# mLSTM scores as five single-pass products: operands split by heads, output gates loaded later

## The chip, the cores and the metric

The kernel runs on one core of one Trainium2 chip. The metric is the device time of one execution in microseconds (us); less is better. Several executions are timed and their median is given, and one execution is profiled, from which the page and the rows below come.

## The reference, cut to what matters

The program is one layer of a hybrid trunk: a big input projection, three groups of heads (latent attention, bidirectional mLSTM, neighbourhood attention), an output projection, and a convolutional feed-forward network. Only the mLSTM heads are touched. There are 4 of them, with 192 features each, 512 latent tokens (the queries) and 768 keys (512 latent, 256 of context):

```python
q = heads(qk[..., :ML_W])                       # B, 4, S, 192
k = heads(qk[..., ML_W:]) * (ML_DH ** -0.5)
...
a = jnp.einsum('bhtd,bhsd->bhts', qc, kc) * w_loc      # scores times decay weights
num = ... + jnp.einsum('bhts,bhsv->bhtv', a, vc)
den = ... + a.sum(axis=-1)
h = num / jnp.maximum(jnp.abs(den), jnp.exp(-m_t))[..., None]
...
return (h.transpose(0, 2, 1, 3).reshape(o.shape) * o)  # output gate, both directions summed
```

The kernel doesn't scan in chunks. It forms each head's whole scores k·q once, multiplies them by the decay weights of both directions, and sums over the keys. Everything is float32. A product of two float32 operands can be made either by TensorE's own float32 matmul, or by splitting each operand in a high part of the reduced type fp32r and a low part (the rest), and summing fp32r products.

## The kernel before, in words

`stage_front` makes the input projection and writes it to DRAM (`proj`, feature rows by 768 tokens). `stage_mix` has `stage_mla` (latent operands) and `stage_heads`, which runs three parts in one block: `one` (a `softmax` of 6 latent heads, 24 units of 128 queries), `two` (`mlstm`), and `three` (`windows`, neighbourhood attention). `stage_tail` then makes the output projection and the feed-forward network. Each engine has its own instruction list, in an order written by hand, and semaphores tie them.

**Units of mLSTM.** `two` has 24 units: head `n // 6`, and within a head the key tiles in `ORDER` (4, 5, 0, 1, 2, 3): two context tiles and four latent ones. Unit n goes like this:

- SyncE, `load_rows(n)` (L1656): two DMAs bring decay rows, broadcast over 128 partitions, from `rrow` into slot n % 5 of `g_ring`. It first waits until unit n - 5 is done (`v_ok`).
- GpSimd adds the causal mask for latent tiles (`mask`, L1681). Within head 2 it also makes the bias slabs of neighbourhood attention (`extra`, L1273), once their tables have landed.
- ScalarE, `weights(n)` (L1702): two exponentials on the slot. `scalar` (L1714) runs it three units ahead; at the last unit of a head it does `scaled` (L1712) after it: four scaled copies out of the accumulators.
- TensorE, `score(n)` (L1795): the 192 features as two float32 matmuls of 96 rows each, 512 queries wide, into one of two banks. It waits for DVE's products of unit n - 2.
- VectorE, `products(n)` (L1760 for context tiles, L1765 for latent ones): score times weights, into the slot.
- TensorE, `values(n)` (L1818): the slot against the values, 8 blocks for a context tile and 5 for a latent one, each 193 columns wide.

TensorE's list is score(n + 2), values(n), and so on. At the end of a head VectorE makes the inverse denominators (`inverse`, L1727 to L1731), ScalarE scales one direction (L1712) and VectorE adds the other (`summed`, L1740); values of the next head wait for both, since they use the same accumulators. Two units later TensorE turns the head (`turn`, L1806), and VectorE multiplies it by the output gates (`gated`, L1751), which `put` stores.

**Loads.** All of these are on SyncE's one queue. At the start of `stage_heads` it loads q and k of all heads (L1169), the values, and the rows of units 0 to 4. When the latent heads are finished it loads the output gates `l_o` (L1180; q, k and gates lie 96 features to a partition set), and then, in a loop over n from 5, the rows of unit n, followed from n = 6 on by two items of `parts` each: neighbourhood q, two halves of k, a window table and eight bias tables `n_slab_wide` (L1195). A bias table is made of runs of 192 bytes.

Of the kernel before, what the change touches and what calls it, by code (L numbers as in the profile page):

```python
# [764 lines left out]
def stage_mix(nc, A, sb, ps, sem, proj, vtok, mix, ones, eps, front, spent, ends, lat, early):  # L765

    rrow = nc.dram_tensor("rrow", [2 * ML_H, KEYT, SEQ], F32, kind="Internal").ap()
    with ExitStack() as ctx:
# [5 lines left out]
        ml = dict(q=arena.at("l_q", [HALF, 2 * ML_H, SEQ], ML_AT + 40960),  # L774
                  k=arena.at("l_k", [HALF, 2 * ML_H, TOK], ML_AT),
# [344 lines left out]
def stage_heads(nc, A, arena, ps, sem, proj, vtok, mix, ident, ones, rqs, rows_st, mla, ml, na, early):  # L1120

    with ExitStack() as ctx:
# [40 lines left out]
        with nc.Block() as block:  # L1163
            @block.sync
            def _(sp):
                sp.wait_ge(rows_st, 32)
                for dst, at, w in ((ml["q"], O_MQ, SEQ), (ml["k"], O_MK, TOK)):
                    r = row_of(at)
                    sp.dma_start(dst[:, :, :], proj[r:r + ML_W, 0:w].rearrange("(a p) t -> p a t", p=HALF)).then_inc(ml_ld, 16)  # L1169
# [10 lines left out]
                sp.dma_start(ml["og"][:, :, :], proj[r:r + ML_W, 0:SEQ].rearrange("(a p) t -> p a t", p=HALF)).then_inc(og_ld, 16)  # L1180
# [8 lines left out]
                for n in range(SLOTS_R, two.UNITS):  # L1189
# [27 lines left out]
            def _(pe):  # L1217
                def to_mlstm(u):
                    if u == 0:
                        pe.wait_ge(ml_ld, 16 * (2 + KEYT))  # L1220
                        pe.wait_ge(one.e_ok, one.UNITS)
# [19 lines left out]
            def _(dve):  # L1241
                one.vector(dve)
# [38 lines left out]
            def _(act):  # L1281
# [9 lines left out]
                one.scalar(act, head_out, drain)  # L1291
# [29 lines left out]
def softmax(nc, arena, at, sem, tag, heads, score, v, scale, ident, lag, s_ps, t_ps, o_ps):  # L1321
# [66 lines left out]
    def vector(dve):  # L1388
# [12 lines left out]
        for u in range(UNITS + lag):  # L1401
# [8 lines left out]
            if u < UNITS:  # L1410
                inverse(u)

# [7 lines left out]
    def scalar(act, head_out, drain):  # L1420
# [17 lines left out]
        for u in range(UNITS + lag):  # L1438
# [8 lines left out]
            if u >= lag:  # L1447
                turn_and_out(u)
        out(heads - 2)
# [153 lines left out]
def mlstm(nc, arena, sem, ml, banks, ident):  # L1603
# [5 lines left out]
    q, k, og, v = ml["q"], ml["k"], ml["og"], ml["v"]  # L1609
# [7 lines left out]
    HALF_BANK = SEQ // 2  # L1617

# [26 lines left out]
    z_ok = sem("g_ones_set")  # L1645
    mk_ok = sem("g_masked")
# [9 lines left out]
    def load_rows(sp, n):  # L1656
# [4 lines left out]
        for d in (1, 0):  # L1661
# [4 lines left out]
            at += w  # L1666

# [38 lines left out]
    def scalar(act):  # L1706
# [46 lines left out]
    def vector(dve):  # L1753
# [14 lines left out]
        for n in range(UNITS):  # L1768
            products(n)
            h, i = n // KEYT - 1, n % KEYT  # L1770
            if h >= 0:
# [3 lines left out]
                elif i == 2:  # L1775
                    gated(dve, h)
        inverse(dve, ML_H - 1)
# [12 lines left out]
    def score(pe, n):  # L1790
# [41 lines left out]
    f.score, f.turn = score, turn  # L1832
    f.tensor, f.vector, f.gpsimd, f.scalar = tensor, vector, gpsimd, scalar
# [1095 lines left out]
```

## Time and profile before

| | us |
|---|---|
| median of 3 timed runs | 2611.5 (2609.99 to 2613.75) |
| profiled execution, its own time | 2612.05 |
| its span in the profile | 2610.4 |
| latent heads (`one`) | 778 to 880 |
| mLSTM (`two`), first score after the latent heads to last values | 880.8 to 975.6 |
| neighbourhood attention (`three`) | 975.6 to 1027 |
| output projection and feed-forward network | 1027 to the end |

The profiled execution's time is 1.65 us more than its span: what lies around it. How the views are read: a row of the timeline is a start, a length, an engine, a line of the kernel, an operation, output and inputs, and how many instructions are merged; brackets give the idle time of that engine just before and what ended it. The start of one group on TensorE to the start of the next is what the group costs; its own length is longer, since matmuls are pipelined. [...] A float32 matmul shows as two records, an fp32r one as one.

### The profile page before, as it was taken

To read this page: it belongs to the slowest core of one execution; us is meant where nothing else is said; L and a number is where in the kernel's file an instruction comes from. 1 tells how busy PE (TensorE), PEld (TensorE's weight loads), DVE (VectorE), ACT (ScalarE), POOL (GpSimd) and SP (SyncE) were. 2 spreads that over 40 slices of the span, in tenths; PEclk is the share of its full clock that TensorE was granted. 3 is DMA by queue.
4 is the path that set the end of the run, shared out by engine and by line. 5 is a ranking of instruction groups with operands and counts; after the bars stand their busy time and mean duration, and the time that the engine had idled before them with its cause. 6 is when DMAs were issued, how large, how long until landed. Compare 5 with 4: busy or idle time off the path is not lost.

```text
span 2610.4 us, 39575 instructions
## 1 busy us (share of the span) xinstructions
PE 2530.5 (97%) x15352; PEld 2184.3 (84%) x15352; DVE 1553.0 (59%) x1811; ACT 932.0 (36%) x1235; POOL 187.8 (7%) x247
## 2 busy tenths in 40 slices
PE   4999999999999998999999999999999999999997
PEld 3788888888756576888899999999999988888886
DVE  5534543474274336337788888888888854333345
ACT  3221212222334334225455555555555532222222
POOL 1000000000106223000000000000000010000000
PEclk9999999999999999999999999999999999999998
DMA  9855555786405554432322322233223262423223
GB/s 367 328 216 214 208 194 196 259 312 231 147 14 138 129 126 160 172 121 93 125 114 109 136 113 112 108 134 115 112 109 133 107 239 88 144 99 133 100 89 109
DMA packets 109081, 401.48 MB, mean 154 GB/s; under 512 B 17512, under 2 KB 37912, under 8 KB 78280
## 3 DMA queue, kind: packets, MB, share of 16 engines
q1 hardware_dynamic: 79328, 294.78, 32.1%
q0 software_dynamic: 15680, 88.28, 9.0%
q10 hardware_dynamic: 14000, 17.44, 1.8%
q8 instruction: 47, 0.77, 0.1%
q14 instruction: 26, 0.21, 0.0%
HBM read 362.22 MB, written 37.45 MB: 153 GB/s over the span
## 4 chain that ended last, share of the span: by engine, by line
PE 56%; DVE 2%; DMA 1%; ACT 1%; issue 0%; POOL 0%; DVEq 0%; ACTq 0%
PE f_ps L2711 25%; PE f_late_ps L2768 13%; PE f_ps L2768 11%; PE f_first_ps L2768 7%; DMA f_raw<-in_w_down 0%; DVE h L2677 0%; PE f_late_ps L2735 0%; PE f_ps L2722 0%; DVE f_lo L2353 0%; DVE x_lo L2529 0%; DVE f_lo L2433 0%; DVE h L2523 0%; PE f_first_ps L2787 0%; DVE f_c L2478 0%; DMA f_raw<-in_w_up 0%
## 5 line engine op out<-in xcount | busy, mean ns | idle before, releaser
L2711 PE MATMUL f_ps<-f_u_hi,f_hi 128*128 128x512 f32 x671 | 262.9, 392 | 1.7 <-DVE f_lo L2353 1.7
L2711 PE MATMUL f_ps<-f_u_hi,f_lo 128*128 128x512 f32 x671 | 262.7, 392 | 0.0
L2711 PE MATMUL f_ps<-f_u_lo,f_hi 128*128 128x512 f32 x671 | 262.5, 391 | 0.0
L2456 DVE SCALAR_TENSOR_TENSOR h<-f_ps,mod,h 128x512 f32<-128x512 f32 (+1 forms) x76 | 57.0, 751 | 316.4 <-PE f_ps L2711 316.4
L619 PE MATMUL i_ps<-hn_hi,i_hi 128*128 128x512 f32 x608 | 240.5, 395 | 0.0
L619 PE MATMUL i_ps<-hn_hi,i_lo 128*128 128x512 f32 x608 | 239.7, 394 | 0.0
L619 PE MATMUL i_ps<-hn_lo,i_hi 128*128 128x512 f32 x608 | 238.5, 392 | 0.0
L2107 ACT ACTIVATE f_hi<-f_raw 128x1408 fp32r<-128x1408 f32 (+1 forms) x82 | 123.0, 1500 | 295.3 <-PE f_ps L2711 274.1
L2433 DVE TENSOR_TENSOR f_lo<-f_s,f_hi 128x1024 fp32r<-128x1024 f32 x160 | 195.5, 1222 | 41.1 <-ACT f_hi L2137 41.1
L493 DVE TENSOR_TENSOR i_lo<-i_raw,i_hi 128x2048 fp32r<-128x2048 f32 x38 | 87.0, 2291 | 218.3 <-ACT i_hi L357 218.3
L2137 ACT ACTIVATE f_hi<-f_s 128x1024 fp32r<-128x1024 f32 x160 | 168.6, 1054 | 80.3 <-PE f_late_ps L2768 36.4
L2353 DVE TENSOR_TENSOR f_lo<-f_raw,f_hi 128x1408 fp32r<-128x1408 f32 (+1 forms) x82 | 145.9, 1779 | 58.2 <-ACT f_hi L2107 57.8
L2137 ACT ACTIVATE f_hi<-f_raw 128x1024 fp32r<-128x1024 f32 x120 | 126.8, 1058 | 131.0 <-PE f_ps L2768 65.4
L2433 DVE TENSOR_TENSOR f_lo<-f_raw,f_hi 128x1024 fp32r<-128x1024 f32 x120 | 146.8, 1224 | 10.5 <-ACT f_hi L2137 9.0
L2711 PEld LDWEIGHTS f_ps<-f_u_hi,f_hi 128*128 128x128 f32 x671 | 126.0, 188 | 30.3 <-DVE f_lo L2353 1.8
L2711 PEld LDWEIGHTS f_ps<-f_u_hi,f_lo 128*128 128x128 f32 x671 | 126.0, 188 | 27.9
L2711 PEld LDWEIGHTS f_ps<-f_u_lo,f_hi 128*128 128x128 f32 x671 | 126.0, 188 | 27.8
L505 DVE SCALAR_TENSOR_TENSOR i_ring<-i_ring,cs 128x2048 f32<-128x2048 f32 x60 | 138.2, 2346 | 0.0
L619 PEld LDWEIGHTS i_ps<-hn_hi,i_hi 128*128 128x128 f32 x608 | 114.2, 188 | 27.7 <-issue 1.7
L2768 PE MATMUL f_ps<-x_hi,f_hi 128*128 128x256 f32 x480 | 135.8, 283 | 1.4 <-DVE f_c L2439 1.4
L2768 PE MATMUL f_late_ps<-x_hi,f_hi 128*128 128x256 f32 x480 | 135.9, 283 | 0.0
L2768 PE MATMUL f_late_ps<-x_lo,f_hi 128*128 128x256 f32 x480 | 135.8, 283 | 0.0
(413 smaller groups left out, 6658.7 us busy)
## 6 DMA issues: line engine op xcount, KB each, us to landing
f_raw<-in_w_up SPq DMA_DIRECT2D x88, 1024.0 KB, 5.1
i_ring<-in_ada_rest POOLq DMA_DIRECT2D x64, 1024.0 KB, 5.3
f_raw<-in_w_down SPq DMA_DIRECT2D x64, 704.0 KB, 4.0
i_raw<-in_w_in SPq DMA_DIRECT2D x38, 1024.0 KB, 4.9
i_ring<-in_ada_first SPq DMA_DIRECT2D x32, 1024.0 KB, 7.4
f_raw<-in_w_out SPq DMA_DIRECT2D x16, 1024.0 KB, 4.9
u_spill<-f_u SPq DMA_DIRECT2D x44, 256.0 KB, 2.1
f_u_raw<-u_spill POOLq DMA_DIRECT2D x44, 256.0 KB, 5.7
```

Of the source, the lines that this page charges most:

```text
L493: nc.vector.tensor_tensor(w_lo[s][:, :, :], raw[s][:, :, :], w_hi[s][:, :, :].bitcast(F32), ALU.subtract).then_inc(lo_ok, 1)
L505: nc.vector.scalar_tensor_tensor(acc[g], ada[g % 2], col, acc[g], ALU.mult, ALU.add).then_inc(ada_ok, 1)
L619: mm = nc.tensor.matmul(pt[s][:, 0:SEQ], w[s][:, k, :], x[:, k, 0:SEQ], **flags)
L2107: nc.scalar.activation(w_hi[s][:, 0:kt, :], raw[s][:, 0:kt, :], ACT.Copy).then_inc(hi_ok, 1)
L2137: nc.scalar.activation(slot_of(w_hi, q), source(par, q), ACT.Copy).then_inc(bh_ok, 1)
L2353: nc.vector.tensor_tensor(w_lo[s][:, 0:kt, :], raw[s][:, 0:kt, :], w_hi[s][:, 0:kt, :].bitcast(F32), ALU.subtract).then_inc(lo_ok, 1)
L2433: nc.vector.tensor_tensor(slot_of(w_lo, q), source(par, q), slot_of(w_hi, q).bitcast(F32), ALU.subtract).then_inc(bl_ok, 1)
L2456: nc.vector.scalar_tensor_tensor(ht, pt[s][:, :], mod[:, bass.ds(group * KT + m, 1), 0:1].rearrange("p a b -> p (a b)"), ht, ALU.mult, ALU ...
L2711: mm = nc.tensor.matmul(pt[s][:, :], m[:, k, :], v(k, slice(0, SEQ)), start=(k == 0 and n == 0), stop=(k == len(ks) - 1 and n == 2))
L2768: mm = nc.tensor.matmul(to[:, 0:HALF_T], w[:, k, :], v, start=(q in (0, 1, 3) and k == 0 and n == 0), stop=(k == HK - 1 and n == 2), skip_ ...
```

## The change

- The score of a unit is five fp32r matmuls, each 128 rows deep and 512 wide. The first 128 features take three: high·high, high·low, low·high. The last 64 features take two: the key's tail is laid twice over the 128 partitions (high in one tile, low in another), and query's high and low tails are stacked in one tile.
- Operands come by heads. `load_operands(h)` makes six DMAs per head (for q and for k: 128 rows, and the 64 tail rows twice). Heads 0 and 1 are loaded at the start of the stage. Head 2 is loaded after the rows of unit 5 (the latent heads' buffers are its place), and head 3 after the rows of unit 9. Between head 3's first query DMA and its other five, SyncE waits until VectorE is finished with head 2's low parts, since the two heads share one tile.
- Per head ScalarE makes four high parts (`operand_high`) and VectorE four low parts (`operand_low`). For heads 0 and 1 they go between the units of the latent heads (`aside`), for head 2 on ScalarE after its iterations 3 to 6 of mLSTM and on VectorE after its iterations 4 to 7, for head 3 after 9 to 12 and 10 to 13.
- The output gates are loaded after the rows of unit 6, rather than ahead of those of unit 5. The neighbourhood loads begin after the rows of unit 11, rather than 6.

```diff
@@ stage_heads, block.sync
-                for dst, at, w in ((ml["q"], O_MQ, SEQ), (ml["k"], O_MK, TOK)):
-                    r = row_of(at)
-                    sp.dma_start(dst[:, :, :], proj[r:r + ML_W, 0:w].rearrange("(a p) t -> p a t", p=HALF)).then_inc(ml_ld, 16)
+                for h in range(2):
+                    two.load_operands(sp, h, proj)
...
-                sp.dma_start(ml["og"][:, :, :], proj[r:r + ML_W, 0:SEQ].rearrange("(a p) t -> p a t", p=HALF)).then_inc(og_ld, 16)
+                gates = (ml["og"][:, :, :], proj[r:r + ML_W, 0:SEQ].rearrange("(a p) t -> p a t", p=HALF), og_ld)
...
-                    if n >= SLOTS_R + 1:
-                        for dst, src, s in parts[2 * (n - SLOTS_R - 1):2 * (n - SLOTS_R)]:
+                    if n == SLOTS_R:
+                        for m in range(2):
+                            sp.wait_ge(one.stored[m], 16 * (MLA_H // 2))
+                        two.load_operands(sp, 2, proj)
+                    if n == SLOTS_R + 1:
+                        sp.dma_start(gates[0], gates[1]).then_inc(gates[2], 16)
+                    if n == SLOTS_R + 4:
+                        two.load_operands(sp, 3, proj)
+                    if n >= SLOTS_R + 6:
+                        for dst, src, s in parts[2 * (n - SLOTS_R - 6):2 * (n - SLOTS_R - 5)]:
                             sp.dma_start(dst, src).then_inc(s, 16)
...
@@ block.vector, block.scalar: called at the end of each unit of the latent heads
+                def aside(u):
+                    if 12 <= u < 20:
+                        two.operand_low(dve, (u - 12) // 4, (u - 12) % 4)
...
+                def aside(u):
+                    if 11 <= u < 19:
+                        two.operand_high(act, (u - 11) // 4, (u - 11) % 4)
...
@@ mlstm
-    ho = [arena.at(f"g_head{n}", [HALF, 2, SEQ], WORK_AT + 10240 + 4096 * n) for n in range(2)]
+    ho = [arena.at(f"g_head{n}", [HALF, 2, SEQ], WORK_AT + 9280 + 4096 * n) for n in range(2)]
...
+    def load_operands(sp, h, proj):
+        for full, dup, at, w in ((parts[h]["q"], parts[h]["qt"], O_MQ, SEQ), (parts[h]["k"], parts[h]["kt"], O_MK, TOK)):
+            r = row_of(at) + h * ML_D
+            sp.dma_start(full[:, :], proj[r:r + P, 0:w]).then_inc(qk_ld[h], 16)
+            if h == ML_H - 1 and w == SEQ:
+                sp.wait_ge(ql_ok, 4 * h)
+            for n in range(2):
+                sp.dma_start(dup[TAIL * n:TAIL * (n + 1), :], proj[r + P:r + ML_D, 0:w]).then_inc(qk_ld[h], 16)
+
+    def operand_high(act, h, n):
+        o = parts[h]
+        to, frm = ((o["k_hi"], o["k"]), (o["q_hi"], o["q"]), (o["kt_hi"], o["kt"]), (o["qt_st"], o["qt"]))[n]
+        if n == 0:
+            act.wait_ge(qk_ld[h], 96)
+        nc.scalar.activation(to[:, :], frm[:, :], ACT.Copy).then_inc(qh_ok, 1)
+
+    def operand_low(dve, h, n):
+        o = parts[h]
+        dve.wait_ge(qh_ok, 4 * h + n + 1)
...
@@ scalar
+            if n in SPLIT_AT:
+                operand_high(act, *SPLIT_AT[n])
+
+    SPLIT_AT = {n: (2, n - 3) for n in range(3, 7)}
+    SPLIT_AT.update({n: (3, n - 9) for n in range(9, 13)})
@@ vector
+            if n - 1 in SPLIT_AT:
+                operand_low(dve, *SPLIT_AT[n - 1])
@@ score
-        for a in range(2):
-            mm = nc.tensor.matmul(s_ps[n % 2], k[:, 2 * h + a, st * P:(st + 1) * P], q[:, 2 * h + a, :],
-                                  start=(a == 0), stop=(a == 1))
+        if n % KEYT == 0:
+            pe.wait_ge(ql_ok, 4 * (h + 1))
+        o, at = parts[h], slice(st * P, (st + 1) * P)
+        terms = ((o["k_hi"], o["q_hi"]), (o["k_hi"], o["q_lo"]), (o["k_lo"], o["q_hi"]), (o["kt_hi"], o["qt_st"]), (o["kt_lo"], o["qt_st"]))
+        for m, (a, b) in enumerate(terms):
+            mm = nc.tensor.matmul(s_ps[n % 2], a[:, at], b[:, :], start=(m == 0), stop=(m == len(terms) - 1))
```

## Rows read from the trace of the kernel before

**Rows 1.** The page's part 1, TensorE and the others: busy us, share, instructions.

```profile
PE 2530.5 (97%) x15352; PEld 2184.3 (84%) x15352; DVE 1553.0 (59%) x1811; ACT 932.0 (36%) x1235; POOL 187.8 (7%) x247
```

**Rows 2.** Stages: stretch, length, busy PE, PEld, DVE, ACT, POOL, clock, DMA, GB/s.

```profile
778.00:866.00 88.00, 86.63 (x378) 57.77 (x378) 38.63 (x93) 37.10 (x71) 50.76 (x23) 1.00 0.41 110
882.00:922.00 40.00, 35.58 (x151) 27.12 (x150) 11.19 (x25) 10.79 (x23) 4.69 (x7) 0.91 1.07 216
```

**Rows 3.** Timeline of TensorE, a score and the values behind it, steady state.

```profile
926.31 1.88 PE L1795 MATMUL m_banks<-l_q,l_k 96*128 96x512 f32 x4
928.03 1.80 PE L1818 MATMUL m_banks<-l_v,g_ring 128*128 128x193 f32 x10
```

**Rows 4.** Stages, L2711 alone (fp32r 128x512): PE, PEld, clock, DMA share, GB/s.

```profile
1100.00:1110.00 10.00, 10.00 (x46) 8.29 (x45) 1.00 0.32 128
```

**Rows 5.** Timeline, turn from head 0 to head 1: all that TensorE waits for.

```profile
902.96 1.88 PE L1795 MATMUL m_banks<-l_q,l_k 96*128 96x512 f32 x4
...
906.74 0.72 POOL L1681 TENSOR_TENSOR g_ring<-g_ring,l_causal 128x256 f32<-128x256 f32 x1 [14.98 <-DMA g_ring<-rrow]
...
909.26 5.29 PE L1818 MATMUL m_banks<-l_v,g_ring 128*128 128x193 f32 x16 [4.42 <-ACT g_part L1712]
...
911.48 0.73 POOL L1681 TENSOR_TENSOR g_ring<-g_ring,l_causal 128x256 f32<-128x256 f32 x1 [4.02 <-DMA g_ring<-rrow]
...
914.40 1.88 PE L1795 MATMUL m_banks<-l_q,l_k 96*128 96x512 f32 x4
```

**Rows 6.** Stages, columns as in rows 2: while k loads; just after that wait.

```profile
897.00:898.50 1.50, 1.50 (x7) 0.90 (x6) 0.32 (x1) 0.45 (x1) 0.00 (x0) 1.00 1.04 416
...
907.50:909.00 1.50, 0.00 (x0) 0.00 (x0) 0.08 (x1) 1.50 (x4) 0.00 (x0) 0.50 1.08 182
```

**Rows 7.** Timeline of SyncE's queue: when DMAs were issued and how long that took.

```profile
891.46 0.43 SPq L1195 DMA_DIRECT2D n_q<-proj  x1
...
896.45 0.84 SPq L1665 DMA_DIRECT2D g_ring<-rrow  x2
...
900.07 6.04 SPq L1665 DMA_DIRECT2D g_ring<-rrow  x2
```

**Rows 8.** DMA issues, 860 to 985: count, KB each, median us to landing.

```profile
g_ring<-rrow SPq DMA_DIRECT2D x19, 256.0 KB, 3.7
...
l_o<-proj SPq DMA_DIRECT2D x1, 1536.0 KB, 9.5
n_k<-proj SPq DMA_DIRECT2D x2, 768.0 KB, 9.9
```

**Rows 9.** Timeline, turn from head 1 to head 2, then score(20) at the next.

```profile
933.02 1.88 PE L1795 MATMUL m_banks<-l_q,l_k 96*128 96x512 f32 x4
...
933.85 1.36 ACT L1712 ACTIVATE g_part<-m_banks,g_den 128x192 f32<-128x192 f32 x4 [1.74 <-DVE g_den L1731]
...
934.74 2.85 PE L1818 MATMUL m_banks<-l_v,g_ring 128*128 128x193 f32 x16
...
935.70 1.22 DVE L1760 SCALAR_TENSOR_TENSOR g_ring<-m_banks,g_ring 128x1024 f32<-128x1024 f32 x1
...
937.42 1.88 PE L1795 MATMUL m_banks<-l_q,l_k 96*128 96x512 f32 x4
...
956.04 1.88 PE L1795 MATMUL m_banks<-l_q,l_k 96*128 96x512 f32 x4
```

**Rows 10.** Timeline of GpSimd in head 2: bias slabs, and the next mask.

```profile
942.01 8.28 POOL L1273 TENSOR_TENSOR n_slab<-n_slab_wide,n_window 128x256 f32<-128x256 f32 x12
...
953.54 0.72 POOL L1681 TENSOR_TENSOR g_ring<-g_ring,l_causal 128x256 f32<-128x256 f32 x1 [3.25 <-DMA g_ring<-rrow]
```

**Rows 11.** Timeline: a high part on ScalarE and a low one on VectorE elsewhere.

```profile
1006.39 1.66 ACT L1312 ACTIVATE x_hi<-x_under_low 128x512 fp32r<-128x512 f32 x3
...
1008.86 1.28 DVE L1255 TENSOR_TENSOR x_lo<-x_under_low,x_hi 128x512 fp32r<-128x512 f32 x2
```

**Rows 12.** Timeline, latent heads: VectorE's shortest wait between two of its units.

```profile
821.06 0.96 DVE L1404 TENSOR_REDUCE a_max<-m_banks 128x1 f32<-128x768 f32 x1 [0.99 <-PE m_banks L1136]
```

More of the change, by code:

```diff
@@ L773, in stage_mix @@
         arena = Arena(nc, nc.sbuf_base - ARENA, ARENA)
-        ml = dict(q=arena.at("l_q", [HALF, 2 * ML_H, SEQ], ML_AT + 40960),
-                  k=arena.at("l_k", [HALF, 2 * ML_H, TOK], ML_AT),
+        k_at = (ML_AT, ML_AT + 12288, 64832, 77120)
+        q_at = [[at + 2048 * n for n in range(4)] for at in (ML_AT + 40960, ML_AT + 49152)]
+        q_at += [[89408, 91456, 93504, 97600], [95552, ML_AT + 75872, ML_AT + 77920, 97600]]
+        parts = [dict(k=arena.at(f"l_k{h}", [P, TOK], k_at[h]), k_lo=arena.at(f"l_k_low{h}", [P, TOK], k_at[h], F32R),
+                      kt=arena.at(f"l_k_tail{h}", [P, TOK], k_at[h] + 3072), kt_lo=arena.at(f"l_k_tail_low{h}", [P, TOK], k_at[h] + 3072, F32R),
+                      k_hi=arena.at(f"l_k_high{h}", [P, TOK], k_at[h] + 6144, F32R),
+                      kt_hi=arena.at(f"l_k_tail_high{h}", [P, TOK], k_at[h] + 9216, F32R),
+                      q=arena.at(f"l_q{h}", [P, SEQ], q_at[h][0]), q_lo=arena.at(f"l_q_low{h}", [P, SEQ], q_at[h][0], F32R),
+                      q_hi=arena.at(f"l_q_high{h}", [P, SEQ], q_at[h][1], F32R),
+                      qt_st=arena.at(f"l_q_tail_stack{h}", [P, SEQ], q_at[h][2], F32R),
+                      qt=arena.at(f"l_q_tail{h}", [P, SEQ], q_at[h][3])) for h in range(ML_H)]
+        ml = dict(parts=parts,
                   og=arena.at("l_o", [HALF, 2 * ML_H, SEQ], ML_AT + 24576),
@@ L1241, in _ @@
             def _(dve):
-                one.vector(dve)
+                def aside(u):
+                    if 12 <= u < 20:
+                        two.operand_low(dve, (u - 12) // 4, (u - 12) % 4)
+                one.vector(dve, aside)
                 two.vector(dve)
@@ L1290, in drain @@
                     two.weights(act, u)
-                one.scalar(act, head_out, drain)
+                def aside(u):
+                    if 11 <= u < 19:
+                        two.operand_high(act, (u - 11) // 4, (u - 11) % 4)
+                one.scalar(act, head_out, drain, aside)
                 two.scalar(act)
@@ L1386, in tensor, with vector @@
         values(heads - 1, tuple(range(KEYT)))
-    def vector(dve):
+    def vector(dve, aside):
         def turned(w):
@@ L1411, in vector @@
                 inverse(u)
+            aside(u)
     def gpsimd(pool):
@@ L1448, in scalar @@
                 turn_and_out(u)
+            aside(u)
         out(heads - 2)
@@ L1608, in mlstm @@
     AHEAD = 3
-    q, k, og, v = ml["q"], ml["k"], ml["og"], ml["v"]
+    parts, og, v = ml["parts"], ml["og"], ml["v"]
     ring, causal, ccol, rrow = (ml[n] for n in ("ring", "causal", "ccol", "rrow"))
@@ L1617, in mlstm @@
     HALF_BANK = SEQ // 2
+    TAIL = ML_D - P
     def acc(d, t):
@@ L1645, in mlstm @@
     z_ok = sem("g_ones_set")
+    qk_ld = [sem(f"g_operands_loaded{h}") for h in range(ML_H)]
+    qh_ok = sem("g_operand_high")
+    ql_ok = sem("g_operand_low")
     mk_ok = sem("g_masked")
@@ L1666, in load_rows @@
             at += w
+    def load_operands(sp, h, proj):
[15 more added lines that the diff above has]
+        dve.wait_ge(qh_ok, 4 * h + n + 1)
+        if n < 3:
+            to, frm, high = ((o["k_lo"], o["k"], o["k_hi"]), (o["q_lo"], o["q"], o["q_hi"]), (o["kt_lo"], o["kt"], o["kt_hi"]))[n]
+            nc.vector.tensor_tensor(to[:, :], frm[:, :], high[:, :].bitcast(F32), ALU.subtract).then_inc(ql_ok, 1)
+        else:
+            to = o["qt_st"][TAIL:P, :]
+            nc.vector.tensor_tensor(to, o["qt"][TAIL:P, :], to.bitcast(F32), ALU.subtract).then_inc(ql_ok, 1)
     def put(sp, h, mix):
```

5 lines of the change are left out of this document (3 added, 2 removed).

## The prediction

> **What bounds the kernel now.** I read the page's busy times first: TensorE is busy 97% of the span [rows 1]. Then the stages: the latent heads are TensorE's too, 86.6 of 88 us. mLSTM's first 40 us are not: from 882 to 922 the DMA engines are full (share 1.07) and the clock is 0.91 on average [rows 2]. So I followed the timeline at the turn from head 0 to head 1. Score(8) starts at 902.96 and takes 1.72, but values(6) starts only at 909.26. It waits for ScalarE's scaled copies, which stand behind weights(8); those wait for the mask, and the mask waits until 906.74 for the rows of unit 8 [rows 5]. These were issued at 896.45, some 10 us earlier [rows 7]; they stood behind neighbourhood q and k, of which k took 9.9 us [rows 8]. [...]
>
> **TensorE's gain.** A score is two float32 matmuls, 926.31 to 928.03 = 1.72 us [rows 3]. A single-pass fp32r matmul of this size costs 10 / 46 = 0.217 us at full clock [rows 4]; five are 1.09. That saves 0.63 per score, 24 x 0.63 = 15.1 us, if nothing else becomes late.
>
> **High and low parts of heads 0 and 1.** A high part of 512 columns takes 1.66 / 3 = 0.55 us, a low one 1.28 / 2 = 0.64 [rows 11]. For 768 columns I take half again as much, 0.83 and 0.96. VectorE's shortest wait between two latent units is 0.99 [rows 12], so each low part fits; ScalarE is busy 37 of 88 us [rows 2]. So they cost nothing. Without that cover it would be the low parts, 4 x 0.96 + 4 x 0.64 = 6.4 us. Their loads meet a DMA share of 0.41 [rows 2], and nobody needs them before the eleventh unit.
>
> **Turns between heads.** The first values of a head wait for the copies: 933.85 plus two copies of 0.34 is 934.53, start 934.74 [rows 9], however short the score before is. So at three turns the saving vanishes, 1.9 us. At the first two, a low part of 768 columns now stands ahead of the products that end at 936.92, 0.50 ahead of the score that needs them [rows 9]. With the high part behind the copies I take 0.9 us each (0.4 to 1.4).
>
> **A new chain.** Here I chose most. ScalarE makes high part j of head 2 (j = 0 to 3) behind weights(6 + j), and VectorE waits for it ahead of products(5 + j). For head 3 it is weights(12 + j) and products(11 + j). Before, products(n) needed weights(n) alone. Now VectorE stops when the rows of the unit after it are late, and score(n + 2) and values(n) stop behind it.
>
> **The queue.** Heads 2 and 3 add 1.28 MB of loads each to the full stretch. No row shows loads of 64 rows. Between the gates' pace (1536 KB in 9.5 us, 165 GB/s [rows 8]) and the pace while k loads (416 GB/s [rows 6]) a head costs 7.8 or 3.1 us of DMA time; I take 3.5, nearer to k, which like them has 128 rows per 768 tokens. It is added work, so it can't bring a gain. The rows of unit 8 landed behind the k issued ahead of them, so I let this queue finish in order. On the clock of before:
>
> - Eight scores save 5.0 us up to the end of head 0: 902.96 becomes 898.0. The rows of unit 6 stand behind head 2's operands and make products(5) 0.5 late: 898.5.
> - Those rows land at about 893; the gates (some 6.5 us of DMA time) stand ahead of unit 7's rows: about 901. Weights(7) 1.3, high 0.55, low 0.64, products(6) 1.2: score(8) begins at 904.5. Denominators and two copies follow; values(6) begin at 906.1 (before 909.26). TensorE was idle 6 us, so the half clock of [rows 6] stays, and they end at 910.8 (before 914.40 [rows 5]). Gain 3.6.
> - SyncE issues the rest of head 3 once VectorE has made head 2's last low part, behind products(7), at about 910.3. The rows of unit 10 and all neighbourhood loads queue behind that wait. Before, q was issued at 891.46 [rows 7] and unit 9's rows, which stood to it as unit 14's do now, were in at 911.5 [rows 5]: 20 us. Now q goes at 912.6, behind some 2 us of head 3's operands: unit 12's rows land at about 925, unit 13's at 929, unit 14's at 934.
> - By the chain products(11) end at 928.8 (weights 1.3, high 0.8, low 1.0, products 0.9). TensorE has been idle 5 us; score(13) and values(11) run partly at half clock, until 934.0. Weights(14) end at 936.0, so values(12) begin at 936.9 and end at 939.5 (before 937.42 [rows 9]). Loss 2.1: all saved so far is spent.
> - Head 2's five scores save 3.1 and its low part at the turn costs 0.9: values(17) end at 956.0, before at 956.04 [rows 9]. The bias tables come five units later, so GpSimd starts its 8.3 us of slabs at about 948 instead of 942.01, and the next mask had only 3.25 us of slack [rows 10]. Unit 20's weights, and the copies behind them, become 1.5 late.
> - Head 3 saves three scores, 1.9. What follows moves as a whole: its loads wait for the last score and the last values, as before.
>
> Sum: 0 + 1.5 - 1.9 = -0.4. Against the profiled execution's own time that is 2612.05 - 0.4 = 2611.6, and the median of the runs lies 0.55 below that execution: **2611.0**.
>
> [...]
>
> **Rivals.**
> Faster: the rows land in time, since the gates no longer stand ahead of unit 5, nor q and k ahead of unit 8, and a quiet queue lands rows in 3.7 us [rows 8]. Against it: 40 us of full DMA [rows 2] get 7 us more work and less time. It gives 15.1 - 1.9 - 1.8 = 11.4, and up to 7 more if the old wait (4.6, and 2.5 of half clock) goes too. Some wait will stay, so I price it at 8: 2603.5.
> Slower: the queue's wait for head 2's low parts decides. If operands load at the gates' pace (7.8 instead of 3.5 us), the rows of units 7 and 12 are 4 us later each, values(12) begin at 941 or later, and the slabs push unit 20 by as much: 6 us slower, 2617. It is slower than before from about 1 us more at each turn.
> It doesn't do what it says: if an fp32r matmul costs what a float32 record does, 1.72 / 4 = 0.43, a score is 2.15 and the kernel 24 x 0.43 = 10 us slower, 2621. Against it stand the 46 in 10 us [rows 4].
>
> **How the numbers follow.** A measurement of this kernel tells about 0.2%, 5.2 us, from no change. My forecast has 0.42 (own range 2606.5 to 2616), faster 0.36, slower 0.18, not as said 0.04. To leave out no more than 2 in 10, the range goes some 3.5 us beyond the first rival's price and just over the second's: 2600 to 2618. Faster 0.36, same 0.42, slower 0.22.
>
> **What the profile would show.** Scores in groups of five, 1.09 us from their start to values. An idle TensorE before score(8) and values(6), and again in head 1 before score(13), released by VectorE's products; clock 0.50 behind both. VectorE waiting for ScalarE ahead of its low parts. SyncE silent from about 896 to 910. If unit 12's rows land within 5 us of issue, the backlog is wrong and the first rival holds. If the latent heads lengthen, the cover is wrong. If the slabs end before unit 20's rows land, that term is nothing.

## The result, and the profile after

The changed kernel takes 2619.37 us (median of 20 runs) against 2613.36 for the kernel before (also 20 runs): ratio 1.0023, 95% interval 1.0017 to 1.0029, 6 us slower. The forecast was 2611.0, within 0.2% of before; the time is just past the upper end of its range. The second rival had the sign and nearly the size (2617).

The stages of the changed kernel (stretch, length, busy TensorE, weight loads, VectorE, ScalarE, GpSimd, with instructions as x, then TensorE's granted clock as a share of full speed, DMA share, GB/s): latent heads, mLSTM, neighbourhood.

```profile
780.50:881.70 101.20, 98.63 (x419) 64.11 (x419) 48.23 (x106) 48.72 (x90) 57.18 (x24) 1.00 0.28 85
881.70:985.10 103.40, 83.50 (x423) 75.54 (x424) 36.76 (x73) 32.30 (x64) 19.91 (x29) 0.92 0.70 170
985.10:1034.70 49.60, 38.93 (x217) 28.66 (x216) 35.11 (x84) 28.94 (x69) 24.87 (x16) 1.00 0.42 138
```

The same three in the kernel before:

```profile
778.40:880.80 102.40, 99.75 (x417) 63.78 (x417) 42.26 (x98) 43.49 (x82) 52.96 (x24) 1.00 0.36 96
880.80:975.60 94.80, 90.38 (x400) 68.51 (x401) 30.36 (x65) 27.73 (x56) 19.88 (x29) 0.96 0.68 159
975.60:1026.90 51.30, 40.61 (x218) 29.32 (x216) 35.13 (x84) 28.94 (x69) 24.86 (x16) 0.97 0.41 131
```

mLSTM grew by 8.6 us, the stages around it gave back 1.2 and 1.7: 5.7 in all, near the 6.0 measured. (The two profiled executions differ by 9.7 us in their spans; the other 4 stand ahead of and behind these stages, 2.1 and 1.9, in code that the change doesn't touch.) Within mLSTM TensorE has 6.9 us less to do, yet it idles 19.9 us instead of 4.4. Seven waits make the idle time. First TensorE's own waits (880 to 986: what waited, for what, us in total, times, longest), then the timeline of the five that matter, 18.5 us of it (start, length, operation, and in brackets the idle time before it and what ended it):

```profile
PE m_banks L1863 <- DVE g_ring L1827: 12.0, 3, 5.7
PE m_banks L1863 <- DVE g_ring L1822: 4.2, 2, 3.7
PE m_banks L1885 <- ACT g_part L1769: 3.6, 2, 2.5
```

```profile
903.17 0.80 PE L1863 MATMUL m_banks<-l_q_high,l_k_high 128*128 128x512 f32 x1 [5.44 <-DVE g_ring L1827]
911.23 0.50 PE L1863 MATMUL m_banks<-l_q_high,l_k_high 128*128 128x512 f32 x1 [3.68 <-DVE g_ring L1822]
936.93 0.80 PE L1863 MATMUL m_banks<-l_q_high,l_k_high 128*128 128x512 f32 x1 [5.73 <-DVE g_ring L1827]
944.13 2.85 PE L1885 MATMUL m_banks<-l_v,g_ring 128*128 128x193 f32 x16 [1.14 <-ACT g_part L1769]
967.24 4.53 PE L1885 MATMUL m_banks<-l_v,g_ring 128*128 128x193 f32 x16 [2.50 <-ACT g_part L1769]
```

Before, TensorE had one stall [rows 5] and none at the second turn [rows 9]. Now scores 7 and 8 wait at the first turn, score 13 and values 12 at the second, values 18 at the third. Behind the stalls stands what released each product:

```profile
899.26 1.33 ACT L1759 ACTIVATE g_ring<-g_ring,l_ccol 128x512 f32<-128x512 f32 x2 [7.64 <-DMA g_ring<-rrow]
900.50 0.82 ACT L1712 ACTIVATE l_k_high<-l_k 128x768 fp32r<-128x768 f32 x1
901.36 0.96 DVE L1720 TENSOR_TENSOR l_k_low<-l_k,l_k_high 128x768 fp32r<-128x768 f32 x1 [9.87 <-ACT l_k_high L1712]
902.23 0.88 DVE L1827 SCALAR_TENSOR_TENSOR g_ring<-m_banks,g_ring 128x512 f32<-128x512 f32 x2
...
907.20 1.33 ACT L1759 ACTIVATE g_ring<-g_ring,l_ccol 128x512 f32<-128x512 f32 x2 [5.88 <-DMA g_ring<-rrow]
```

Read it from the first bracket on: ScalarE waited 7.64 us for rows, the high part stands behind it, VectorE waited 9.87 us for that, and only then came the products. Rows of unit 6 landed at 899.2, those of unit 7 at 907.2. SyncE's queue shows when they were issued:

```profile
886.68 1.72 SPq L1700 DMA_DIRECT2D l_q<-proj  x1
...
891.34 1.06 SPq L1694 DMA_DIRECT2D g_ring<-rrow  x2
892.44 0.43 SPq L1207 DMA_DIRECT2D l_o<-proj  x1
892.91 5.65 SPq L1694 DMA_DIRECT2D g_ring<-rrow  x6
898.61 0.43 SPq L1700 DMA_DIRECT2D l_q<-proj  x1
916.68 1.09 SPq L1704 DMA_DIRECT2D l_q_tail<-proj  x2
...
926.40 4.33 SPq L1212 DMA_DIRECT2D n_slab_wide<-in_rpb  x2
930.79 6.98 SPq L1694 DMA_DIRECT2D g_ring<-rrow  x2
```

Rows 6 took 7.9 us and rows 7 13 to 14, where the median before was 3.7 [rows 8]. From 899 to 916.7 SyncE stands at its wait for head 2's low parts, and the DMA engines run dry behind it (share 0.00). The stretch in which rows are late, and the idle one:

```profile
893.00:907.20 14.20, 8.76 (x41) 7.75 (x40) 1.76 (x3) 2.06 (x3) 0.00 (x0) 0.88 1.05 254
909.50:917.00 7.50, 5.77 (x22) 5.29 (x23) 6.61 (x14) 3.97 (x9) 0.00 (x0) 0.77 0.00 0
```

### The profile page after: what moved, and what is told of

It is laid out like the page before. It is cut to its first block, busy times and chain, and to the rows that moved or that the text cites. A ratio compares the mean times of both kernels' runs of the same rounds, so it can differ in the third digit from the quotient of the medians.

```text
span 2620.1 us, 39681 instructions
## 1 busy us (share of the span) xinstructions
PE 2524.4 (96%) x15376; PEld 2193.1 (84%) x15376; DVE 1565.4 (60%) x1827; ACT 941.9 (36%) x1251; POOL 192.1 (7%) x247
## 4 chain that ended last, share of the span: by engine, by line
PE 56%; DVE 2%; DMA 1%; ACT 1%; issue 0%; POOL 0%; DVEq 0%; ACTq 0%
PE f_ps L2779 25%; PE f_late_ps L2836 13%; PE f_ps L2836 11%; PE f_first_ps L2836 7%; DMA f_raw<-in_w_down 0%; DVE h L2745 0%; PE f_late_ps L2803 0%; PE f_ps L2790 0%; DVE f_lo L2421 0%; DVE x_lo L2597 0%; DVE f_lo L2501 0%; DVE h L2591 0%; PE f_first_ps L2855 0%; DVE f_c L2546 0%; DMA f_raw<-in_w_up 0%
## 5 line engine op out<-in xcount | busy, mean ns | idle before, releaser
L619 PEld LDWEIGHTS i_ps<-hn_lo,i_hi 128*128 128x128 f32 x608 | 114.1, 188 | 26.0
```

The costliest lines, as they stand in the source:

```text
L619: mm = nc.tensor.matmul(pt[s][:, 0:SEQ], w[s][:, k, :], x[:, k, 0:SEQ], **flags)
```

## The experiments

The kernel before was timed beside each; its median lay between 2612.6 and 2613.7. A result is a median, then its ratio to the kernel before with the 95% interval. Differences are of medians, and where the ratios tell another thing, it is said.

### What the scores are worth, and what the queue costs

**pure_gain**: the new scores without the loads and parts of heads 2 and 3, on the queue of before. Its output is not the reference's.

```
-                pe.wait_ge(ql_ok, 4 * (h + 1))
-        o = parts[h]
+                pe.wait_ge(ql_ok, 4 * (h % 2 + 1))
+        o = parts[h % 2]
```

> Scores alone: the five fp32r matmuls, but all four heads' scores use the operands of heads 0 and 1, so the loads and the high and low parts of heads 2 and 3 are left out (their scores are not the reference's), and the queue issues gates and neighbourhood loads where the kernel before does. Theory (late rows and the chain ScalarE to VectorE ate the gain): mLSTM shrinks by 15.1 - 1.9 = 13 us, 2600 against 2613.4; at the first turn the old wait stays and grows by what TensorE arrives earlier. Rival (the five matmuls save less than 1.09 to 1.72, or the parts made in the latent heads cost there): under 5 us faster.

2603.64 us, ratio 0.9967 (0.9955 to 0.9979): 9.7 faster. Between the two theories. mLSTM takes 84.4 us, 10.4 less, with 7.2 us still waited for scaled copies, 6.4 of them at values(6). The kernel before waits 4.4 there. So TensorE's own time shrank by 13.2, as the theory had it (from 90.4 to 77.2 us busy), and 2.8 of that went into a longer wait for the same late rows.

**before_with_queue**: the new queue without the scores.

```
+    if n == SLOTS_R: <wait for the stores>; load_operands(2)
+    if n == SLOTS_R + 1: <output gates>
+    if n == SLOTS_R + 4: load_operands(3)
-    if n >= SLOTS_R + 1: <neighbourhood, two loads>
+    if n >= SLOTS_R + 6: <neighbourhood, two loads>
```

> The queue alone: float32 scores as before, but SyncE also makes the operand loads of heads 2 and 3 (into tiles that nobody reads), gates and neighbourhood loads stand where the change puts them, and there is no wait for low parts and no high or low part. Theory: rows are later, but without the chain VectorE isn't stopped, and units are 0.6 us longer, so between 3 us faster (the old wait at the first turn goes) and 4 slower; 2614. Rival (the loads themselves cost it all, chain or not): TensorE idle as long as in the changed kernel, 12 us or more slower than before, 2625.

2618.45, ratio 1.0019 (1.0010 to 1.0028): 5.1 slower, further than the 4 my theory allowed. The queue alone costs almost what the whole change costs, with waits of 3.85 and 2.30 us at the first two turns. It was then taken apart: **before_loads_only** keeps its two `load_operands` and no move, **before_moves_only** the two moves and no load.

> The kernel before (scores in fp32, no parts), plus only the twelve operand loads of heads 2 and 3, into tiles that nobody reads, where the changed kernel issues them; the output gates' load and the neighbourhood's loads stay where the kernel before has them. The whole queue of the changed kernel cost it 5.1 us. Theory: the 2.5 MB of operand loads are the price, since they stand ahead of rows 6 and 10 on the queue: 2617 us, 4 us above the kernel before. Rival: the moves (the gates behind rows 6, the neighbourhood's tables five units later) are the price, and the loads fit in the idle share of the DMA engines: within 1.5 us of the kernel before.

2615.07, ratio 1.0006 (0.9997 to 1.0014). Neither: 1.7 above, between the two theories.

> The kernel before, with only the moves of the changed kernel's queue: the output gates' load behind rows 6 instead of ahead of rows 5, the neighbourhood's loads five units later; no operand loads. Theory: with no operand loads in front of them the gates stand in nobody's way, and rows 5 and 6 come 2 to 4 us earlier than in the kernel before, which takes the 4.4 us stall at values(6) down: 2610 us, 3 us below the kernel before. Rival (the moves are the price): 2617 us, 3 to 5 us above it.

2612.48, ratio 0.9996 (0.9988 to 1.0005), 0.9 below: not told from no change. So 1.7 and -0.9 apart, but 5.1 together (each of the three is known to about 2 us, so the excess is likely and not certain). The turn to head 1 shows how little each alone changes; values(6) in the kernel with the loads only, then in that with the moves only (before: [rows 5]):

```profile
910.60 4.48 PE L1839 MATMUL m_banks<-l_v,g_ring 128*128 128x193 f32 x16 [6.00 <-ACT g_part L1733]
```

```profile
908.33 2.85 PE L1832 MATMUL m_banks<-l_v,g_ring 128*128 128x193 f32 x16 [1.55 <-ACT g_part L1726]
933.62 4.33 PE L1832 MATMUL m_banks<-l_v,g_ring 128*128 128x193 f32 x16 [2.10 <-ACT g_part L1726]
```

The moves cleared the first turn (4.42 became 1.55) and made a new wait at the second, 2.10, with values that last 4.33 at a clock of 0.65, for 2.85 at the first: neighbourhood q, k and tables now stand ahead of units 12 to 17 instead of 7 to 12. With the operand loads added, both turns are late (the 3.85 and 2.30 above).

### The wait for the low parts

**own_tile**: head 3's query tail goes to a free tile, so that SyncE needn't wait.

```
-        q_at += [..., [95552, ML_AT + 75872, ML_AT + 77920, 97600]]
+        q_at += [..., [95552, ML_AT + 75872, ML_AT + 77920, 44032]]
-            if h == ML_H - 1 and w == SEQ:
-                sp.wait_ge(ql_ok, 4 * h)
```

> The changed kernel, but head 3's query tail has a tile of its own and SyncE doesn't wait for head 2's low parts. Theory: the queue's silent stretch (898.6 to 916.7) goes; unit 10's to 14's rows come up to 15 us earlier, the idle 5.7 us before score(13) and most of what follows it goes, the first idle stretch (5.4 and 3.7 us) stays: 6 us faster than the changed kernel, 2613. Rival (DMA bandwidth, not the silent stretch): the same stall only moves, within 2 us of 2619.

2613.60, ratio 1.0002 (0.9993 to 1.0011): 5.8 below the changed kernel. As the theory said. The wait is worth the whole net loss: without it the change is neutral. But TensorE's gain is still spent, and the stalls of the first turn are still there (5.73 and 3.50 us).

**own_tile_lag**: on top, VectorE makes its low parts three units behind ScalarE's high parts (`if n - 3 in SPLIT_AT` for `n - 1`).

> As own_tile, and VectorE makes each low part three units behind ScalarE's high part instead of one, so that it waits for no rows that its own products don't need. Theory: the waits of VectorE for ScalarE ahead of low parts (16.9 + 8.8 us in the changed kernel) vanish, and the idle time before score(7) with them; what is left is the copies at the first turn: 7 us faster than own_tile, 2606. Rival (the chain only shows what late rows cost anyway): within 2 us of own_tile.

2613.89, ratio 1.0003 (0.9994 to 1.0012). My theory fell. The stalls moved, they didn't shrink (15.1 us in all for 15.4); TensorE's largest wait is now the one that the kernel before has:

```profile
PE m_banks L1883 <- ACT g_part L1767: 14.9, 3, 7.3
```

The chain over the parts is only where late rows show first.

### The bursts

**after_gates_first** undoes one move of the changed kernel.

```
+    <output gates>
     for n in range(SLOTS_R, two.UNITS):
-        if n == SLOTS_R + 1: <output gates>
```

> The changed kernel with one part undone: the output gates are loaded ahead of rows 5 again, as before. The trace of the changed kernel shows no DMA traffic from the end of the latent heads to rows 5 (some 4 us), and rows 7 land 13 us after their issue, behind the gates. Theory: the 1.5 MB then use the idle stretch and leave the queue of rows 6 to 8; rows 7 land 4 us earlier: 2616 us, 3 us below the changed kernel (2619.4). Rival: they delay rows 5, the operands of head 2 and rows 6 by as much as they took from rows 7: within 1.5 us of 2619.4.

2616.61, ratio 1.0013 (1.0004 to 1.0021), 2.8 below the changed kernel, where the theory had put it; but the two intervals overlap (1.0017 to 1.0029 there), so the gain is likely and not certain. The trace goes the theory's way: rows 8 are in at 903.1, in the changed kernel at 908.0. So moving the gates later seems to have cost time, since it left the DMA engines idle when the latent heads ended (share 0.00 from 884.0 to 885.5, against 0.96 with the gates first) and put 1.5 MB ahead of rows 7.

**spread_loads** issues the same bytes evenly and, like own_tile, without the wait (a load stands behind the rows whose number is its key, 0 ahead of them all; head 3's parts are made one unit later):

```
+    AFTER = {0: k and its tail of head 2, 5: q and its tail of head 2, 6: gates 0, 7: q of head 3,
+             8: gates 1, 9: k of head 3, 10: its tail, 12: gates 2, 14: gates 3}
```

> The changed kernel with the same bytes in another order: no wait of SP on low parts (head 3's query part and both heads' raw tails in tiles of their own); key operands of head 2 issued at once when the latent heads end; its query operands behind rows 5; the gates in four loads of one head each, behind rows 6, 8, 12 and 14; head 3's operands behind rows 7, 9 and 10; head 3's parts made one unit later. Theory: the loss is the burst that rows 6 to 8 queue behind, not the bytes: no rows land later than 7 us after issue, the stalls at units 6 to 8 go down to those of the kernel with no loads (2603.6), and the time is 2607 us, 6 below the kernel before. Rival: the bytes themselves cost it, wherever they stand in this stage: 2612 us or more, within 2 us of the changed kernel without SP's wait (2613.6).

2609.47, ratio 0.9982 (0.9973 to 0.9990): 9.9 below the changed kernel with the same bytes, 4.1 of it beyond own_tile, though 2.5 short of what I expected. In its timeline the first turn is clean, the second is not (and values(18) wait 2.70 us at the third):

```profile
901.74 2.85 PE L1900 MATMUL m_banks<-l_v,g_ring 128*128 128x193 f32 x16 [0.70 <-ACT g_part L1783]
...
926.85 0.79 PE L1878 MATMUL m_banks<-l_q_high,l_k_high 128*128 128x512 f32 x1 [5.68 <-DVE g_ring L1837]
```

L1837 makes the products of context tiles, so this is score(14), released by products(12). They stand behind head 3's first low part, its high part behind weights(13), and these behind rows 13. In the queue:

```profile
912.85 0.99 SPq L1700 DMA_DIRECT2D g_ring<-rrow  x2
913.90 2.56 SPq L1218 DMA_DIRECT2D n_slab_wide<-in_rpb  x2
916.50 5.27 SPq L1700 DMA_DIRECT2D g_ring<-rrow  x2
```

```profile
922.61 1.33 ACT L1773 ACTIVATE g_ring<-g_ring,l_ccol 128x512 f32<-128x512 f32 x2 [5.20 <-DMA g_ring<-rrow]
```

The first of them are rows 13: they went out in 1 us, behind neighbourhood q, k, the window and a gate, and landed at 922.6, about 9 us later. Only rows 14, which took 5.3 us to issue, stand behind the pair of bias tables. I had miscounted: what the next expectations call rows 12 to 14 are rows 14 to 16, and the stall that they call score(13) is score(14). So the pair of tables was not ahead of the rows that made the stall. On the reading that they hold the queue, one load a unit was tried, on the new kernel and, alone, on the one before (in brackets the number of the load: 0 is neighbourhood q, 1 and 2 are k, 3 the window, 4 to 11 the tables):

```
spread_tables      TABLE_AT = {8 + i: (3 + i,) for i in range(ROWS + 1)}, and {17: (0,), 18: (1,), 19: (2,)}
before_tables_one  parts[n - SLOTS_R - 1:n - SLOTS_R] for parts[2 * (n - SLOTS_R - 1):2 * (n - SLOTS_R)]
```

> The kernel with the spread loads (2609.5), and the neighbourhood's eight bias tables, in which each contiguous piece is 192 bytes, one behind each of rows 9 to 16 instead of two behind each of rows 12 to 15, and its query and keys behind rows 17 to 19. In the trace of the spread loads rows 12, 13 and 14 took 5.3, 3.8 and 4.1 us to issue, each behind a pair of tables, and the one long stall left (5.7 us, score(13)) waits for rows 12. Theory: pairs of tables hold the queue; one at a time leaves room, and the stall goes: 2605 us, 4 below the spread loads. Rival: the tables cost what they cost wherever they stand, and earlier they meet the operands of head 3 as well: 2610 us or more.

> The kernel before, with one of the neighbourhood's twelve loads behind each of rows 6 to 17 instead of two behind each of rows 6 to 11; nothing else. In its trace rows 9 and 10 took 6.0 and 3.2 us to issue behind pairs of tables, but no unit of it waited for rows 9 or later. Theory: it changes no wait of TensorE, since the fp32 scores leave the rows that much slack: within 1 us of the kernel before (2613.4). Rival: the stall at values(6) (4.4 us) is partly the tables', and goes down: 2611 us.

2606.71 (0.9973, 0.9964 to 0.9982) and 2607.59 (0.9976, 0.9967 to 0.9985). The first is near its theory's time (2605) for another reason than it gave, as the stall stayed. The second refutes me: the kernel before gains 5.8 us from nothing but one load a unit instead of two. Whether the tables or the second half of k made the difference isn't told apart, as both now come later. Its stall at values(6), 4.42 us and then a clock of 0.50 [rows 6], is now

```profile
907.61 2.85 PE L1818 MATMUL m_banks<-l_v,g_ring 128*128 128x193 f32 x16 [0.71 <-ACT g_part L1712]
```

In the new kernel the gain was 2.8, and the stall at score(14) stayed (6.1 us): with tables from rows 9 on, they fall on head 3's operands, and rows 13, issued at 914.1, landed at 924.2. The DMA engines are full then, at less than half the rate of [rows 6] (stages of spread_tables, columns as above):

```profile
910.00:915.00 5.00, 5.00 (x31) 4.57 (x30) 2.88 (x6) 0.96 (x2) 0.72 (x1) 1.00 1.12 171
915.00:920.00 5.00, 5.00 (x29) 4.66 (x28) 0.89 (x2) 1.39 (x3) 0.00 (x0) 1.00 1.18 172
```

The last step moves the neighbourhood's loads late (tables behind rows 10 to 17, its 2.5 MB of q and k behind rows 18 to 20), on three kernels:

```
+    TABLE_AT = {10 + i: (4 + i,) for i in range(ROWS)}
+    TABLE_AT.update({9: (3,), 18: (0,), 19: (1,), 20: (2,)})
```

> The changed kernel with head 3's query tail in a tile of its own and no wait of SP (2613.6), and with the neighbourhood's loads late: its window behind rows 9, one of its eight tables behind each of rows 10 to 17, its query and keys (2.5 MB) behind rows 18, 19 and 20, instead of two loads behind each of rows 11 to 16. The operand loads of heads 2 and 3 and the gates stay in their bursts. Its trace shows stalls of TensorE of 5.7 and 3.5 us in head 1's turn (rows 7 and 8, behind the operands of head 2 and the gates) and of 1.0, 2.4, 1.1 us in head 2's turn with 2.6 us of values at half clock. Theory: two bursts, two stalls; this takes away the second one only: 2608.5 us, 5 us less. Rival: the operand loads of head 3 behind rows 9 make the second stall by themselves: 2613 us.

> The kernel with the spread loads (2609.5), with head 3's operands behind rows 7, 8 and 9, the gates of heads 1, 2 and 3 behind rows 11, 15 and 18, and the neighbourhood's loads late: window behind rows 9, one table behind each of rows 10 to 17, query and keys behind rows 18 to 20. With the tables at rows 9 to 16 (2606.7) the DMA engines were full from 895 to 930 us at 170 to 280 GB/s and one stall of 6.1 us was left at score(13). Theory: that stall is the tables' and head 3's operands on top of each other; apart, it goes: 2601 us, 5 to 6 us below. Rival: tables at one a unit fill the queue wherever they are (about 170 GB/s at full share), and the stall moves to a later row: 2606 us, no gain.

> The kernel before, scores in fp32, with the neighbourhood's loads late as in the other two (window behind rows 9, one table behind each of rows 10 to 17, query and keys behind rows 18 to 20). One load a unit instead of two gave 2607.6. Theory: of that gain most came from taking the 2.5 MB of query and keys off the stretch behind rows 6 and 7; they are out of it here entirely: 2606 us, and the new scores on an equally ordered queue are worth some 5 us. Rival: tables and keys meet the rows later instead: 2609 us or more.

2612.40 (0.9996, 0.9987 to 1.0004), 2605.67 (0.9977, 0.9967 to 0.9987) and 2606.88 (0.9973, 0.9962 to 0.9984). For the first the rival holds: 1.2 us gained, not 5. For the second too: its stalls moved instead of going, 3.4 us at score(14) and 3.6 at values(18). For the third the theory holds. The mLSTM stage of the third and of the second:

```profile
881.50:969.40 87.90, 87.89 (x401) 66.19 (x402) 30.34 (x65) 27.97 (x56) 19.93 (x29) 1.00 0.63 172
```

```profile
879.10:968.90 89.80, 81.21 (x423) 74.11 (x423) 36.31 (x73) 33.15 (x65) 21.25 (x29) 0.94 0.75 196
```

With fp32 scores and an ordered queue TensorE never waits in this stage and the clock never falls: 87.9 us. With the new ones TensorE is busy 6.7 us less and idle 8.6 us more. The two kernels are the same within their intervals (1.2 us apart by the medians, 1.0 the other way by the ratios); both beat the kernel before, and the changed one by about 13 us.

**pure_gain_late_tables**, the same lines in pure_gain, asks whether it is the operand loads that take the gain.

> The kernel of the pure gain (2603.6: five products on parts of heads 0 and 1 for all four heads, no operand loads or parts of heads 2 and 3, gates first; output not the reference's), with the neighbourhood's loads late: window behind rows 9, one table behind each of rows 10 to 17, query and keys behind rows 18 to 20. The kernel before gained 5.8 to 6.5 us from that (2606.9). Theory: so does this one: 7.2 us of stalls at TensorE were left in it, 6.4 of them at values(6) behind late rows; 2598 us, 9 below the kernel before on the same queue. Rival: on an ordered queue the scores give no more than the changed kernel with both bursts spread showed (2605.7 against 2606.9), since the rows' own path sets the pace: 2603 us or more.

2603.74, ratio 0.9962 (0.9949 to 0.9976). The rival's time holds: the late order gave nothing to a kernel without operand loads. Its first turn is clean (0.42) and the second carries the largest of three waits, 7.9 us in all:

```profile
924.50 4.35 PE L1879 MATMUL m_banks<-l_v,g_ring 128*128 128x193 f32 x16 [4.75 <-ACT g_part L1764]
```

```profile
911.17 0.43 SPq L1207 DMA_DIRECT2D n_slab_wide<-in_rpb  x1
913.12 1.41 SPq L1689 DMA_DIRECT2D g_ring<-rrow  x2
914.57 0.43 SPq L1207 DMA_DIRECT2D n_slab_wide<-in_rpb  x1
```

```profile
921.97 0.72 POOL L1733 TENSOR_TENSOR g_ring<-g_ring,l_causal 128x256 f32<-128x256 f32 x1 [13.99 <-DMA g_ring<-rrow]
```

These are rows 14, on which the copies wait through weights(14): issued by 914.5, landed at 922.0. By the medians five products are worth 3.1 us on this queue without their loads and 1.2 with them; by the ratios 2.9 and -1.0. The intervals overlap, so neither is told from zero, out of the 13.2 that TensorE saves in this stage. What follows is argued, not tested: rows are requested every 2.8 us instead of 3.4, so five ring slots give them less time to land, and the tables alone are enough to make them late.

### The form of a load

**spread_joined** fetches each tail by one load with the step over the two copies outermost, **spread_joined_rows** with the rows outermost.

```
-            for n in range(2):
-                sp.dma_start(dst[TAIL * n:TAIL * (n + 1), :], <64 rows>)
+            sp.dma_start(dst[:, :], [[0, 2], <64 rows>, <columns>])    # spread_joined
+            sp.dma_start(dst[:, :], [<64 rows>, [0, 2], <columns>])    # spread_joined_rows
```

> The kernel with the spread loads (2609.5), with the 64 feature rows that are loaded twice fetched by one load of 128 partitions instead of two of 64: four loads a head instead of six, the same bytes. Theory: the price of the operands is in their bytes and place; fewer loads save 4 issues of 0.55 us of a queue that is not late there: 2609 us, within 1 us of the spread loads. Rival: loads of 64 partitions are the slow ones, and joining them brings rows 9 to 12 forward: 2606 us.

2624.94, ratio 1.0043 (1.0029 to 1.0056): 15.5 us worse with the same bytes in fewer loads. Neither theory. Between 899.5 and 903.5 nothing else seems to run, and the share (last but one) is 0.14 at 51 GB/s:

```profile
899.50:903.50 4.00, 0.00 (x0) 0.00 (x0) 0.00 (x0) 0.00 (x0) 0.00 (x0) 0.95 0.14 51
```

> The joined kernel (2624.9, 15.5 us above the spread loads), in which one load of 128 partitions goes over the 64 feature rows twice (outermost step: which of the two copies); here the same load goes row by row and takes each row twice (outermost step: the row), the same bytes, the same number of loads. The two copies of a row then lie in neighbouring partitions, so the tails' parts are multiplied in a wrong pairing: the output is not the reference's, the work is the same. In the trace of the joined kernel the DMA share stands at 0.50 and the rate at 145 to 151 GB/s for 10 us (897 to 907), with rows 8 issued in 7.4 us. Theory: a load whose outermost step has only two values runs on half of the DMA engines; with 64 values it is spread again, and the time is that of the spread loads or a little below: 2609 us. Rival: it is the reading of one row twice, or four loads of 128 partitions in place of six, that is slow: 2620 us or more.

2609.24, ratio 0.9984 (0.9975 to 0.9993). The order of the steps accounts for the whole loss; but the "half of the engines" of my theory was wrong, read off a mixed stretch. 0.14 of 16 engines is 2.2, about two; that this is one for each value of the outermost step is my estimate from this row, and no other number of values was tried in between.

## Why the prediction was wrong

In short: the forecast failed at the DMA time of a head's operands, and for a smaller part at the wait behind the bias slabs. The stage began 0.9 us later in this profile, which I add to the times of the prediction. It ended 9.0 us later than that forecast (985.1 for 976.1): 6.3 of that stood at values(12), 0.7 came at the start of values(18) and 1.5 in their slower clock (0.60).

- **TensorE's gain**: nearly right, by two errors that cancel. Five products take 1.23 to 1.31 us from their start to the values, not 1.09, since the first takes 0.31 to 0.38 and the others 0.23, against 10 / 46 = 0.217 [rows 4]. But the values behind them also take less, 1.49 us to the next score where the kernel before has 929.66 - 928.03 = 1.63:

```profile
957.71 0.53 PE L1863 MATMUL m_banks<-l_q_high,l_k_high 128*128 128x512 f32 x1
...
959.00 1.79 PE L1885 MATMUL m_banks<-l_v,g_ring 128*128 128x193 f32 x10
960.49 0.53 PE L1863 MATMUL m_banks<-l_q_high,l_k_high 128*128 128x512 f32 x1
```

  So a unit takes 2.78 us instead of 3.35 or 3.36, 0.58 less for the 0.63 forecast, and pure_gain's 13.2 us agree with the forecast's 15.1 - 1.9. Why the values take less isn't shown. Next to nothing of the miss lies here.
- **Parts of heads 0 and 1**: right. The latent heads are 1.2 us shorter (two scores made there, each 0.45 less, make 0.9 of it), VectorE and ScalarE busy 6 and 5 us more beside TensorE. A part of 768 columns took 0.83 and 0.96, as estimated; of 512 columns 0.62 and 0.69, a little over the 0.55 and 0.64.
- **The queue** is where it failed, at its first term. I put a head's operands at 3.5 us of DMA time and had rows 6 land at 893; they landed at 899.2, 5.3 us later than that on this clock. Rows 7, behind the gates, followed at 907.2 for 901.9: again 5. The stretch in which the operands came ran at 225 to 254 GB/s, where I had taken the 416 of k's stretch [rows 6], and q's issue alone took 1.72 us. A part of the miss is no DMA time at all: SyncE took from 886.68 to 891.34 to issue the six loads, with the DMA share at 0.67 from 887 to 891.5, so rows 6 were issued some 2 us after their slot was free (score(4), behind values(1), starts at 889.14). Everything behind inherits this: score(8) 911.2 for 905.4, values(6) 912.6 for 907.0, SyncE's restart 916.7 for 911.2, rows 12 at 933.0 for 925.9, values(12) 944.1 for 937.8. The mechanism of these two turns stands link by link; the one term was 5 us short. That SyncE's wait stands in the chain is shown by own_tile: without it the time is 5.8 us less. The signs named agree with a backlog: rows 12, issued at 922.65, took 10 us to land, and in the first burst the small load stayed behind the large one (the gates landed 13.7 us after their issue, about 906, and rows 7 behind them at 907.2).
- **The slabs**: the wait came as forecast, and larger. It was the second failed step. GpSimd began its slabs at 956.4 where I had 948.9, and ended them at 964.7; the masks of units 20 and 21 stand behind them without a wait for rows, so the slabs and not the rows held them:

```profile
956.41 8.34 POOL L1293 TENSOR_TENSOR n_slab<-n_slab_wide,n_window 128x256 f32<-128x256 f32 x12
964.71 1.41 POOL L1738 TENSOR_TENSOR g_ring<-g_ring,l_causal 128x256 f32<-128x256 f32 x2
```

  Values(18) then start 2.2 us later than a clean turn has them (1.72 behind the start of the score), for the 1.5 forecast, and take 4.23 us instead of 2.68 at a mean clock of 0.60, which I had at nothing.
- **The neighbourhood's loads**: priced at nothing but the slabs. At rows 12 that was a small error here: they came 7.1 us late, 5.5 of it SyncE's late restart. Elsewhere it is large: two of them a unit cost the kernel before 5.8 us (before_tables_one). I had seen q and k ahead of unit 8 and used it for the faster rival, but in their new place I only let them queue behind SyncE's wait and gave them no DMA time ahead of rows 12 to 14, of which rows 14 took 7.0 us to issue.
- **The first rival** (rows in time) fell: even with no operand loads 7 us of waits stay. Its 11.4 would have needed a queue that no order tried here gave. The 2.5 us that it gives the old slower clock are in the rows: values(6) took 5.14 us (909.26 to 914.40, mean clock 0.52) [rows 5], values(12) 2.68 (934.74 to 937.42, clock 1.00) [rows 9].
- **The second rival** was right in mechanism and sign, and 2.4 us low. It supposed 4 us more at units 7 and 12; it was 5 and 7. I gave it 0.18, since I took the price from the row that looked alike (128 rows a load) and not from the row that stood in the same crowd, the gates at 165 GB/s.
- The range missed by 1.4 us: its end was set just over this rival's price, and the rival was 2.4 low.

Open: how much of the 5 us at rows 6 is the 64-row loads, how much the time to issue six of them, and how much the crowd around them. spread_joined_rows, with loads of 128 rows, came out as spread_loads did, so the form costs nothing that could be measured once the queue is spread; in the burst it wasn't tried.

## What to carry to other kernels

When a stage lives on small loads that come in time, price each added load by what the queue does where it will stand, at the rate of the crowded rows, and see which small loads stand behind it; saving compute in such a stage shortens the time that the loads have (argued here, not tested by itself). Look at the queue first: one load a unit instead of two gave 5.8 us for a line of code, and on a queue so ordered the new arithmetic with its loads gave nothing more that could be told (2605.67 against 2606.88). And a wait on a queue that issues for many is worth a tile of its own to avoid (5.8 us here, own_tile).

## What the runs showed of the hardware that I hadn't expected

- Beside the bias tables (192 bytes a piece) the DMA engines were full and moved less. In spread_tables the share is 1.12 to 1.18 at 171 GB/s, against 1.04 at 416 in [rows 6]; in pure_gain_late_tables, where only rows and tables are on the queue from 915 to 920, it is 1.22 at 132 GB/s. Tables alone weren't measured, so that the small pieces are the cause is a guess.
- A load whose outermost step has two values ran at 51 GB/s and share 0.14 (spread_joined, 899.5 to 903.5); the same bytes with the rows outermost cost 15.7 us less in the whole kernel.
- Single-pass products of one score didn't run at the 0.217 us of a long series [rows 4]: 0.23 each and 0.31 to 0.38 for the first. The values behind them were 0.14 us faster per unit than behind float32 scores (1.49 for 1.63).
